# Decoder block with a mixture of experts on one core: the passage from mixer to experts rearranged

## The reference

```
hn   = rms_norm(x, norm_mix)
proj = hn @ w_in + b_in                      # mLSTM heads and gated convolution read it
x    = x + concat(y_mlstm, y_conv) @ w_out
hn2  = rms_norm(x, norm_ffn)                 # needs the mean of squares of each row
group = argmax(hn2 @ w_group + b_group); two experts of the 8 of that group
weights = softmax(two logits) * softmax(group logits)[group]
moe  = sum over the two experts of weight * (silu(hn2 @ w_gate) * (hn2 @ w_up)) @ w_down
out  = rms_norm(x + moe, norm_final)
```

## Time and profile before

| | us |
|---|---|
| median of 3 runs | 1828.26 (1827.84 to 1829.36) |
| the profiled execution | 1829.41 |
| its span, first to last instruction | 1827.7 |

### The profile page before, as it was taken

How to read it: one execution, slowest core, us unless ns; L and a number is a source line. 1 busy time by engine, 2 the same in 40 slices (tenths; PEclk the granted TensorE clock), 3 DMA queues, 4 the chain that set the end, 5 groups by cost and what they waited for, 6 DMA issues and landing times.

```text
span 1827.7 us, 28959 instructions
## 1 busy us (share of the span) xinstructions
PE 1807.3 (99%) x10499; PEld 1453.7 (80%) x10499; DVE 824.4 (45%) x1772; ACT 292.8 (16%) x732; POOL 588.9 (32%) x668
## 2 busy tenths in 40 slices
PE   9999999999999999999999999999999999999997
PEld 8888668888478886688884877788888888888875
DVE  5556755476652767554764761522212212212221
ACT  2022120211211211202111111111111111111111
POOL 5933212044130234120440223234333333333332
PEclk9999999999999999999999999999999999999998
DMA  7642722314522326223133498888888888888874
GB/s 300 225 164 70 267 103 93 127 70 162 184 93 80 141 70 235 112 93 124 73 139 140 156 364 306 325 339 331 329 316 330 316 333 307 333 328 328 330 287 162
DMA packets 81712, 392.30 MB, mean 215 GB/s; under 512 B 17707, under 2 KB 18003, under 8 KB 48784
## 3 DMA queue, kind: packets, MB, share of 16 engines
q1 hardware_dynamic: 50576, 310.49, 45.9%
q0 software_dynamic: 25632, 58.90, 8.7%
q10 hardware_dynamic: 5360, 21.03, 2.9%
HBM read 356.10 MB, written 60.86 MB: 228 GB/s over the span
## 4 chain that ended last, share of the span: by engine, by line
PE 93%; POOL 3%; issue 1%; DMA 1%; DVE 1%; ACT 0%; POOLq 0%; SPq 0%; DVEq 0%; ACTq 0%
PE ps_proj L701 24%; PE ps_proj L1121 6%; PE ps_proj L1123 6%; PE ps_proj L730 6%; PE ps_state L1142 6%; PE ps_num L1142 6%; PE ps_proj L742 5%; PE ps_rows L1121 3%; PE ps_scores L1123 3%; PE ps_rows L1123 3%; PE ps_scores L1121 3%; PE ps_scores L730 3%; PE ps_proj L763 2%; PE ps_num L1149 2%; PE ps_state L730 2%; PE ps_num L1052 1%
## 5 line engine op out<-in xcount | busy, mean ns | idle before, releaser
L1121 PE MATMUL ps_proj<-hnT,wo 128*128 128x128 f32 (+3 forms) x992 | 201.2, 284 | 0.0
L1123 PE MATMUL ps_proj<-hnT,wo 128*128 128x128 f32 (+3 forms) x992 | 199.4, 283 | 0.0
L1121 PEld LDWEIGHTS ps_proj<-hnT,wo 128*128 128x128 f32 x992 | 154.6, 191 | 13.6 <-issue 13.6
L1123 PEld LDWEIGHTS ps_proj<-hnT,wo 128*128 128x128 f32 x992 | 153.9, 191 | 0.0
L701 PE MATMUL ps_proj<-hnT,ww 128*128 128x256 f32 x640 | 151.6, 380 | 0.0
L701 PEld LDWEIGHTS ps_proj<-hnT,ww 128*128 128x128 f32 x640 | 119.3, 190 | 16.8 <-issue 1.4
L1537 POOL TENSOR_TENSOR xres<-ww 128x512 f32<-128x512 f32 x12 | 15.2, 1267 | 291.9 <-DMA ww<-in_w_slots 274.3
L1121 PE MATMUL ps_scores<-hnT,wo 128*128 128x128 f32 (+3 forms) x496 | 99.7, 283 | 0.0
L1123 PE MATMUL ps_rows<-hnT,wo 128*128 128x128 f32 (+3 forms) x496 | 99.7, 283 | 0.0
L1123 PE MATMUL ps_scores<-hnT,wo 128*128 128x128 f32 (+3 forms) x496 | 99.7, 283 | 0.0
L1121 PE MATMUL ps_rows<-hnT,wo 128*128 128x128 f32 (+3 forms) x496 | 99.7, 283 | 0.0
(11 more groups left out here) (516 smaller groups left out, 3558.2 us busy)
## 6 DMA issues: line engine op xcount, KB each, us to landing
wo<-in_w_gu SPq DMA_DIRECT2D x128, 1024.0 KB, 7.2
ww<-in_w_slots SPq DMA_DIRECT2D x43, 1024.0 KB, 4.8
og<-in_w_dn SPq DMA_DIRECT2D x32, 1024.0 KB, 4.9
vx<-in_w_dn SPq DMA_DIRECT2D x32, 1024.0 KB, 7.5
xin<-in_x SPq DMA_DIRECT2D x16, 512.0 KB, 6.2
ww<-w_v_sums SPq DMA_DIRECT2D x16, 512.0 KB, 3.4
xres<-in_x SPq DMA_DIRECT2D x16, 512.0 KB, 6.0
x_rows<-x ACTq DMA_DIRECT2D x16, 512.0 KB, 5.1
```

The costliest lines, as they stand in the source:

```text
L1121: pe.matmul(GU[m][:, 0:n_], wo[:, kt, m * P:(m + 1) * P], xT[:, kt, 0:n_], start=(kt == 0), stop=(kt == KT - 1), skip_group_check=True)
L1123: mm = pe.matmul(GU[m][:, CAP:CAP + n_], wo[:, kt, FF + m * P:FF + (m + 1) * P], xT[:, kt, 0:n_], start=False, stop=(kt == KT - 1), skip_g ...
```

## The change

Five edits, all in the passage:

1. ScalarE squares tile 15 right after its store, ahead of the copies of its transpose.
2. The normalised rows of tiles 14 and 15 are no longer made by VectorE in one instruction each. ScalarE multiplies with the root (`scaled_rows`), GpSimd with the norm weights, after it has issued the first gather.
3. Slot codes and weights lie side by side in one PSUM bank. The early table is still made in two parts, the late one in one part of 64 columns (`late_table`).
4. `unread(12)` becomes `unread(5)`.
5. On VectorE the late weights are made ahead of the places and one-hot tiles, and the first sum of the sorting (L2694) stands behind the copies of the table.

```
-            def half_table(i): ...        # codes, 32 columns, into TABLE
-            def half_weights(i): ...      # weights, 32 columns, into SC, stored_slots(1, SC) first
+            def half_products(i, n, cols_):
+                first = (2 * TL * i + n) * 2 * NE
+                for part_, at in enumerate((slice(0, P), slice(P, SLOTS))):
+                    to = 2 * NE * part_
+                    mm = pe.matmul(TABLE[:, to + cols_.start:to + cols_.stop], hot_half[i][:, n // TL, n % TL, at],
+                                   tok_w[:, first + cols_.start:first + cols_.stop],
+                                   start=False, stop=(n == 2 * TL - 1), skip_group_check=True)
+            def late_table():
+                pe.wait_ge(S_("table_rows_ready"), 4)
+                for n in range(2 * TL):
+                    if n == TL:
+                        pe.wait_ge(S_("hot_ready"), 2)
+                    mm = half_products(1, n, slice(0, 2 * NE))
+                mm.then_inc(S_("table_turned"), 1)
...
                     if kt == FIRST_TABLE:
-                        half_table(1)
-                    if kt == FIRST_TABLE + 1:
-                        half_weights(1)
+                        late_table()
...
-            unread(12)
+            unread(5)
             main_transposes(0)
             half_ranks(1)
             first_gate_up()
...
+                def scaled_rows(i):            # ScalarE
+                    act.wait_ge(S_("rs2_ready"), NTILE + i)
+                    act.wait_ge(S_("ss2_ready"), NTILE + i)
+                    own_instruction(act)
+                    act.activation(hn2[i][:], x2[i][:], ACT.Copy, scale=st2[:, i, 1:2]).then_inc(S_("ss2_ready"), 1)
...
                 store_residual(3)
+                squares_of(3)
                 with act.If(b > NB - 2):
+                    scaled_rows(0)
                     router_act(NTILE - 1)
                     own_instruction(act)
-                squares_of(3)
...
                     logits_turned(NTILE - 1)
+                    scaled_rows(1)
                     store_rows(2)
...
             pool.wait_ge(S_("items_made"), ITEMS["main_rows"])
             gather_main(idx[:, 0:1])
+            for i in range(2):
+                pool.wait_ge(S_("ss2_ready"), NTILE + i + 1)
+                pool.wait_ge(S_("hn2_ready"), NTILE - 2 + i)
+                pool.tensor_tensor(hn2[i][:], hn2[i][:], gffn, ALU.mult).then_inc(S_("hn2_ready"), 1)
...
                     early.rows_weight()
-                    normed_rows(2)
...
+            last.weights()
+            last.rows_weight()
             last.place()
             last.one_hot()
-            last.weights()
-            last.rows_weight()
-            dve.wait_ge(S_("hn2_stored1"), 16 * (2 * (NB - 1) + 1))
-            dve.wait_ge(S_("rs2_ready"), NTILE + 1)
-            dve.scalar_tensor_tensor(out=hn2[1][:], in0=x2[1], scalar=st2[:, 1, 1:2], in1=gffn, op0=ALU.mult,
-                                     op1=ALU.mult).then_inc(S_("hn2_ready"), 1)
...
-            then(dve.tensor_reduce(rank_e.unsqueeze(2), perm3, AX.X, ALU.add))
             dve.wait_ge(S_("table_turned"), TABLES["whole"])
...
-            dve.wait_ge(S_("table_turned"), TABLES["weights"])
-            then(dve.tensor_copy(wgt_e, SC[:, 0:NE]))
-            then(dve.tensor_copy(wgt4_e, SC[:, NE:2 * NE]))
+            then(dve.tensor_copy(wgt_e, STA[:, 1, NE:2 * NE]))
+            then(dve.tensor_copy(wgt4_e, STA[:, 1, 3 * NE:4 * NE]))
             dve.sem_inc(S_("items_made"), 1)
+            then(dve.tensor_reduce(rank_e.unsqueeze(2), perm3, AX.X, ALU.add))
             second_item()
```

More of the change, by code:

```diff
@@ L274, in build @@
         ITEMS = {"main_rows": 1, "items": 2, "weights": 3, "second": 4, "order": 5, "sorted": 6, "visits": 7, "overflow": 8}
-        TABLES = {"early": 1, "whole": 3, "weights": 4}
+        TABLES = {"early": 1, "whole": 3, "early_weights": 2}
         gfin = ww[1][:, 0:D]
@@ L854, in _, with stored_slots @@
             TABLE = STA[:, 1, :]
[L856 to L862, removed]
+            def stored_slots():
                 pe.wait_ge(S_("slots_loaded"), 16 * (1 + TQ))
                 pe.wait_ge(S_("out_read"), out_read(NB - 1, 1, "u3"))
-                stored_slots(0, TABLE)
@@ L868, in half_products @@
-            def half_products(i, n, o, bank):
-                first = (2 * TL * i + n) * 2 * NE + o * NE
+                for i, part_ in enumerate((slots_main, slots_tail)):
+                    pe.matmul(TABLE[:, 2 * NE * i:2 * NE * (i + 1)].rearrange("p (o e) -> p o e", o=2), ident[:],
+                              part_[:].rearrange("p e o -> p o e"), start=(i == 0), stop=False, skip_group_check=True)
+            def half_products(i, n, cols_):
+                first = (2 * TL * i + n) * 2 * NE
@@ L870, in half_products @@
                 for part_, at in enumerate((slice(0, P), slice(P, SLOTS))):
-                    mm = pe.matmul(bank[:, part_ * NE:(part_ + 1) * NE], hot_half[i][:, n // TL, n % TL, at],
-                                   tok_w[:, first:first + NE], start=False, stop=(n == 2 * TL - 1), skip_group_check=True)
-                return mm
-            def half_table(i):
+                    to = 2 * NE * part_
+                    mm = pe.matmul(TABLE[:, to + cols_.start:to + cols_.stop], hot_half[i][:, n // TL, n % TL, at],
+                                   tok_w[:, first + cols_.start:first + cols_.stop],
+                                   start=False, stop=(n == 2 * TL - 1), skip_group_check=True)
@@ L877, in half_table, with early_tokens @@
+                return mm
+            def early_tokens():
+                pe.wait_ge(S_("table_rows_ready"), 1)
                 for n in range(2 * TL):
-                    if n == 0:
-                        pe.wait_ge(S_("table_rows_ready"), 2 * i + 1)
                     if n == TL:
-                        pe.wait_ge(S_("hot_ready"), 1 + i)
-                    mm = half_products(i, n, 0, TABLE)
+                        pe.wait_ge(S_("hot_ready"), 1)
+                    mm = half_products(0, n, slice(0, NE))
@@ L883, in half_table, with early_weights @@
                 mm.then_inc(S_("table_turned"), 1)
[L885 to L889, removed]
+            def early_weights():
+                pe.wait_ge(S_("table_rows_ready"), 2)
                 for n in range(2 * TL):
-                    mm = half_products(i, n, 1, SC)
+                    mm = half_products(0, n, slice(NE, 2 * NE))
+                mm.then_inc(S_("table_turned"), 1)
@@ L1015, in _ @@
                         elif p == 1 and i == 4 and b == NB - 1:
-                            out_part(b, p, i, OUT_BANK[bank], new, {1: stored_codes, 2: lambda: router_turn(NB - 1, CT - 2)})
+                            out_part(b, p, i, OUT_BANK[bank], new, {1: stored_slots, 2: lambda: router_turn(NB - 1, CT - 2)})
                         else:
@@ L1033, in _ @@
             router_rows(NTILE - 2)
-            half_table(0)
+            early_tokens()
             router_turn(NB - 1, CT - 1)
@@ L1039, in _ @@
             router_rows(NTILE - 1)
-            half_weights(0)
+            early_weights()
             GU = [PROJ[:, 0, :], PROJ[:, 1, :], SC[:], RB[:]]
@@ L2693, in _ @@
                                    ALU.is_gt))
-            then(dve.tensor_reduce(rank_e.unsqueeze(2), perm3, AX.X, ALU.add))
             dve.wait_ge(S_("table_turned"), TABLES["whole"])
-            then(dve.tensor_copy(tail_c[:, 0:1], STA[:, 1, NE:NE + 1]))
+            then(dve.tensor_copy(tail_c[:, 0:1], STA[:, 1, 2 * NE:2 * NE + 1]))
             decoded(none4[:, 0:1], tail_c[:, 0:1], 1, pad[:, 1:2], other[:, 0:1])
@@ L2700, in _ @@
             then(dve.tensor_copy(main_e, STA[:, 1, 0:NE]))
-            then(dve.tensor_copy(tail_e, STA[:, 1, NE:2 * NE]))
-            dve.wait_ge(S_("table_turned"), TABLES["weights"])
-            then(dve.tensor_copy(wgt_e, SC[:, 0:NE]))
-            then(dve.tensor_copy(wgt4_e, SC[:, NE:2 * NE]))
+            then(dve.tensor_copy(tail_e, STA[:, 1, 2 * NE:3 * NE]))
+            then(dve.tensor_copy(wgt_e, STA[:, 1, NE:2 * NE]))
+            then(dve.tensor_copy(wgt4_e, STA[:, 1, 3 * NE:4 * NE]))
             dve.sem_inc(S_("items_made"), 1)
+            then(dve.tensor_reduce(rank_e.unsqueeze(2), perm3, AX.X, ALU.add))
             second_item()
```

## The result

The changed kernel is slower: 1831.63 us against 1828.86 (medians of 20 runs each), ratio 1.0014, 95% interval 1.0008 to 1.002. By the ratio that is 2.6 us (the medians themselves lie 2.8 apart), where +1.6 was forecast. The forecast median was 1829.8; 0.6 of the distance to 1831.63 is the kernel before, whose median is 1828.86 over 20 runs and was 1828.26 over the 3 that the forecast started from. The profiled execution took 1831.69, its span 1829.9 against 1827.7.

A forecast was written before the change was run, and what follows sets the result against it. The chain that ended last lay 93% on TensorE. Gate products +1.6, late table -1.7 and low clock +1.7 gave +1.6 on 1828.26, stated as 1829.8 us; the forecast case's own range was 1828.8 to 1831.5, the whole range ended at 1832.0.

The forecast's parts named there:

- the gate products without the clock's part: First expert's gate products on TensorE: the mask, late through GpSimd's hold on the sorting, starts them 1.6 us later.
- the late table: Inside TensorE's gate products: one group of 16 records of 64 columns replaces two groups, 1.7 us less.
- The low clock: TensorE after its wait for the mask: the clock falls to 1.2 GHz, costing 1.7 us, bounds 0 to 3.5.
- the second held instruction: VectorE's sorting: L2012 arrives at 1025.0, is held by GpSimd's second product and is done at 1027.2.
- the two sizes for the hold: VectorE's sorting beside GpSimd: 2.5 us late if held to each instruction's end, or measured delays of 0.47 and 0.81.
- The pause of 4.5: TensorE has no work from the transposes' end at 1027.7 until the ranks at 1032.2, 4.5 us.
- a start stretch of 3.6 us: Kernel's start, at the lower clock: 17 records took 3.61 us, 0.212 each; such a stretch costs 1.7.
- the decode behind the table: Behind the late table: the first tail's and second expert's gathers come 1.3 to 3 us later, but stay hidden.
- the first (held, but the clock stays up, 1828.1): Rival at the pause before the ranks: sorting held, clock not falling, 1828.1 us; chance 0.25.
- The second, a small hold: Rival at VectorE's sorting: GpSimd holds it little or misses it, 1824.9 us, or 1826.1 with measured delays; chance 0.20.
- The third, a long low clock: Rival at the gate products after the pause: over 0.2% slower from 7.9 us of low clock; chance 0.10.

The follow-up runs named there:

- e5: The kernel before with one change, tile 15 squared right after its store: 1828.21 us, ratio 0.9995 to before.
- e11: The changed kernel with each of GpSimd's two products cut into 8 pieces of 128 columns: 1830.78 us, ratio 1.0008 to before.
- e6: The changed kernel with GpSimd's two products held back until the last one-hot tiles, stores after the gathered rows' copies: 1831.16 us, ratio 1.001 to before.
- e4: The kernel before with one change, rows scaled on ScalarE and multiplied on GpSimd behind the first gather: 1836.04 us, ratio 1.004 to before.
- e7: The changed kernel with 18 unread products between the transposes of the gathered rows and the ranks: 1829.75 us, ratio 1.0004 to before.
- e10: The changed kernel with the first sum of the sorting put back ahead of the wait for the late table: 1831.81 us, ratio 1.0017 to before.
- e1: The changed kernel with the normalised rows of tiles 14 and 15 given back to VectorE: 1826.63 us, ratio 0.9992 to before.
- e8: The changed kernel with normalised rows back on VectorE and the sorting's sum ahead of the late table's wait: 1828.74 us, ratio 0.9996 to before.

## Why the prediction was right, step by step

The direction and the mechanism held, and of the three terms of the sum two: the gate products without the clock's part (+1.5, +1.6 forecast) and the late table (-1.8, -1.7 forecast). The low clock was sized too small, and a fourth term, behind the passage, was not in the sum. The whole, 2.6, is 1.0 above the forecast, inside its range; the two misses add up, and no other error hides them. (1828.26 + 1.6 rounds to 1829.9, not 1829.8.)

- Edit 1: the gather was expected at 1021.15 and seen at 1020.92. As forecast its gain was gone, because the mask was late next; e5 shows the mask as the bound even with nothing held.
- Edit 2: L2012 (now L2026) was expected to be the second held instruction. It slipped in beside the first, and the one behind it (L2027) was held, to 1026.96. The border was right: 1027.2 was forecast. The mask came 2.3 later by distance from the store (2.5 forecast). Of the two sizes for the hold, the whole rest of a GpSimd instruction and the short delays of the earlier trace rows, the first was right: e11 and e6 show it. The trace agrees with the lock for a whole instruction that the Trainium skill states ("SBUF — State Buffer", section "SBUF: two separate sides"), except for the first 0.7 of e4's hold of 3.11, which began before GpSimd's product did.
- Edit 3: a gain of 1.7 was forecast. From the table to the first tail it took 8.9 instead of 10.7, a gain of 1.8.
- Edit 4: this is the term that was mis-sized. The pause of 4.5 was 4.3, and the clock fell. The price was read from a start stretch of 3.6 us; here the clock was low beside 4.6 us of work, which cost 2.2 (ranks 0.6, gate products 1.6), not 1.7. e7 gives the same 2.2 back. The low stretch was 6.8 us long in all four profiles with a pause of 3.0 to 4.8 (changed kernel, e4, e10, e11), so what it cost was the part of it that lay beside work: 2.2 here, 3.1 in e4 and in e11.
- Edit 5: the decode behind the table was said to be hidden, and the gathers are (no wait at the first tail or the second expert in the changed kernel), though they were issued 3.7 and 3.4 later by distance from the store, more than the 1.3 to 3 forecast; the second had 0.6 in hand. But the prediction followed VectorE's late work only to those gathers. It ends in the second expert's hidden product, 0.6 on TensorE. This step was missing.

The table of distances adds up to the measured time. The gate products start 2.1 later (1.7 by the mask, on the ranks' start, and 0.4 in the ranks themselves), the way from them to the table is 1.5 longer, the way from there to the first tail 1.8 shorter, and behind the passage 0.6 is lost: +2.5 by the profile's points, and +2.6 by the ratio.

Of the rivals, the first (held, but the clock stays up, 1828.1) is what e7 builds; its 1.0004 is 0.9 above that, of which 0.5 is the unforecast last column. The second, a small hold, is ruled out by the 1.20 and the 2.25. The third, a long low clock, didn't come: it was low for 6.8 us, with 4.6 beside work, short of the 7.9 that it needed.

## What to carry to other kernels

Before work goes to GpSimd "because it is idle", look at what VectorE does beside it: a chain of tiny two-input instructions pays the rest of each GpSimd instruction, whatever its own size. If it must be there, cut it into short pieces or put it where VectorE waits anyway: both brought the mask forward here (e11, e6), though neither kernel was shown to be faster than before. When a wait is taken from TensorE, ask which wait is next, how long the new pause is, and whether there are still products to fill it; and follow a late engine past the passage, to the first place where the bound engine needs it.

## What the runs showed of the hardware

- A VectorE product on 8 columns took 0.17 alone and up to 3.11 beside GpSimd's 128x1024 products (2.4 each). One-input reductions between them kept 0.16. In e4 the hold of 3.11 began 0.7 before the start of the GpSimd product with which it ended, while the gather was being issued; other instructions beside such an issue took their usual 0.17. That was not settled.
- With a pause of 1.5 us and 5 unread products ahead of it, the clock stayed up in e1 and fell in e8 and e6, there 1.7 and 0.7 after TensorE had resumed. The pause before the change, 1.55 behind 12 unread products, left it up. Whether a pause of this length costs 1.6 differs between profiles of the same order of work.
- The low stretch lasted 3.4 us in e8 and e6, and 6.8 in the changed kernel, e4, e10 and e11. TensorE was idle for its first 2.2 in the changed kernel and for its first 0.4 in e11.
